# GpSimd computes the low half of 100 of the 504 weight pieces, where VectorE computed all of them

## The chip, the cores and the metric

The kernel runs on one core of one Trainium2 chip. The metric is the device time of one launch in microseconds (us). The names of the engines in the profile are PE (TensorE, matrix multiply) with PEld (its weight load), DVE (VectorE), ACT (ScalarE), POOL (GpSimd) and SP (SyncE, which here only starts DMAs).

## What is computed

Two transformer-like blocks run one after the other on 256 tokens of width 2048, all in float32. Of the reference only the products with large weights matter here:

```
# first block, twice (l = 0, 1)
mod = c_act @ w_mod[l] + b_mod[l]            # one row times 2048 x 6144
h = rmsnorm(x, norm_gain[l]) * (1.0 + scale) + shift
proj = h @ w_in[l]                           # 256 x 2048 times 2048 x 7504
...                                          # sparse attention, retention, gates
x = x + gate * (y @ w_out[l])                # 256 x 2048 times 2048 x 2048
# second block, once
h = concat([meta_tokens (16), x, pad])
proj = rms_norm(h, norm_mix) @ w_in_2        # 2048 x 7176
...                                          # stick-breaking and forgetting attention
h = h + merged @ w_out_2
q = rms_norm(h, norm_ffn) @ peer_w_query     # 2048 x 2048
...                                          # top-k, gather of 16384-row tables peer_u, peer_v
```

## The kernel before, in words

A float32 product is made from rounded halves. A weight piece `raw` is split into a high half `hi`, rounded to the engine's fp32r type, and a low half `lo = raw - hi`. The activations are split the same way (`hH`, `hL`). TensorE then makes three products for each pair: wH with hH, wL with hH, wH with hL (all at L1818, a helper that records every matmul; L1821 records the transposes).

**Seven passes.** `PIECES` lists the weight pieces: pass 0 (`w_in[0]`, 128 pieces), 1 (`w_out[0]`, 32), 2 (`w_in[1]`, 128), 3 (`w_out[1]`, 32), 4 (`w_in_2`, 120), 5 (`w_out_2`, 32) and 6 (`peer_w_query_2`, 32), together 504. A piece is 256 rows of the weight by a group of columns, mostly 512 wide, and lies in SBUF as 128 x 1024. Eight pieces (`pc` 0 to 7) make one column group.

**The road of a piece k.** SP loads it into `ring` (`NS` = 4 slots). ACT copies it, rounded, into `wH[k % 3]` (L626); for that it waits until TensorE has finished piece k - 3 (`"cut used"`, `NB` = 3 buffers). DVE subtracts into `wL[k % 3]` (L1130), which gives `"lo"` to TensorE and `"ring used"` to SP. In pass 4 the 16 meta tokens read some groups (keys and values of both attentions, and the last 344 columns) straight from the raw piece, so there `"ring used"` comes from TensorE.

**The order.** `order()` is one list of steps that every engine walks, each picking what concerns it. After TensorE's piece q comes the split of piece q + 3 (`splits`), then one or more steps of three lanes (`pump`): X (sparse attention, gates), Y (retention) and M (`mods`, the modulation rows). DVE carries most of the lane work between its splits. An engine's queue is strictly in order, so a lane step behind a split waits for it. The mods step on DVE (L1286) multiplies a 128 x 1024 piece of `w_mod` by a column of c and adds it to an accumulator in `UHM`. TensorE does so for pieces 0 to 63 of the 192, DVE for pieces 64 to 191; the latter are loaded by POOL (L2371, into `P` or `SY`, three slots), where the load of piece m + 3 stands at the same step as the use of piece m and waits for that use (`"mod used"`).

**POOL before the change** only starts DMAs: inputs, `w_mod`, the decay tables of the retention (L2347), and in the last part, from about 1800 us on, the indirect gathers of expert rows (L2361). In that last part DVE takes a dot product of each gathered 128 x 2048 tile of `peer_u` (L1777), and TensorE mixes the rows of `peer_v`.

Of the kernel before, what the change touches and what calls it, by code (L numbers as in the profile page):

```python
# [9 lines left out]
ALU = mybir.AluOpType  # L10
ACT = mybir.ActivationFunctionType
F32 = mybir.dt.float32
# [56 lines left out]
class Marks:  # L69
# [9 lines left out]
    def tick(self, sem, *names):  # L79
        self.n[sem] += 1  # L80
        return self._named(sem, 1, names)
# [13 lines left out]
    def at(self, *name):  # L95
        if self.counting:
            return None, 0
        sem, n = self.names[name]
        return self.handles[sem], n
# [60 lines left out]
PIECES = [[(n, c0, w, pc) for n, (c0, w) in enumerate(g) for pc in range(8)] for g in GROUPS]  # L160
NB, NS, NG = 3, 4, 11
# [3 lines left out]
def meta_part(c0, w):  # L165

    for a, b in ((SK, MSK), (SV, MSV), (FK, MFK), (FV, MFV)):
        if a <= c0 < a + 1024:
            return 0, b + c0 - a
    if c0 + w > FL:  # L170
        return FL - c0, MFL
    return None


def order():
# [198 lines left out]
def mixer_peer_program(nc, I, out):  # L374
    with ExitStack() as ctx:
# [8 lines left out]
        ring = sb("ring", [128, NS, 1024])  # L384
# [34 lines left out]
        handles = {}  # L419
        for name in ("pe_piece", "pe_turned", "pe_bias", "pe_side",  # L420
                     "act_hi", "act_stored", "act_x", "act_y", "act_h", "act_side",
                     "dve_lo", "dve_stored", "dve_x", "dve_y", "dve_h", "dve_side",
                     *[f"mod_in{i}" for i in range(11)], "const_in", "pos_in", "x_in", "meta_in", "forget_in", "ffn_in", "decay_in", "turned_in", "out_done", "out_act_done",
                     *[f"ring_in{i}" for i in range(NS)], *[f"expert_in{i}" for i in range(NG)]):
            handles[name] = sem(name)
# [66 lines left out]
        def heads(v, n):  # L492
            return v.rearrange("p (h n) -> p h n", h=n)
# [606 lines left out]
        def vector(e, w):  # L1100
# [20 lines left out]
            def split(p, q):  # L1121
                n, c0, wd, pc = PIECES[p][q]
                r, k = next(loads), next(cut)
                raw = heads(ring[:, r % NS, 0:2 * wd], 2)
                hi, lo = (heads(b[k % NB][:, 0:2 * wd], 2) for b in (wH, wL))
                w.wait_ge(*at("hi", k))
                names = [("lo", k)]
                if not (p == 4 and meta_part(c0, wd)):
                    names.append(("ring used", r))
                tt(lo, raw, hi.bitcast(F32), ALU.subtract).then_inc(*tick("dve_lo", *names))  # L1130
# [581 lines left out]
            for what, *a in order():  # L1712
# [41 lines left out]
                elif what == "meta":  # L1754
                    p, q = a
# [585 lines left out]


        def gpsimd(e, w):
            gathers = itertools.count()

            def load(sem, to, src, *names):
                e.dma_start(to, src).then_inc(*landed(sem, *names))  # L2347

            def gather(tab, picks):
                n = next(gathers)  # L2350
                slot, before = SLOTS[n]
                if before is not None:
                    w.wait_ge(*at("expert used", before))
                elif slot in (3, 4):
                    w.wait_ge(*at("turned x"))
                    w.wait_ge(*at("hidden", slot - 3))
                elif slot == 5:
                    w.wait_ge(*at("lo", LAST_CUT))
                elif slot == 7:
                    w.wait_ge(*at("grouped", 6, 3))  # L2360
                e.indirect_dma_start(gs[slot], None, tab[0], bass.IndirectOffsetOnAxis(ap=picks, axis=0)).then_inc(  # L2361
                    *landed(f"expert_in{slot}", ("gathered", n)))

            def mod_load(m):
                l, c0, k = m // 96, m // 16 % 6 * 1024, m % 16
                b, before = mod_slot(m)
                if before is not None:
                    w.wait_ge(*at("mod used", before))
                if m in (64, 160):
                    w.wait_ge(*at("chunk", 2 * l if m == 160 else 0, 3))  # L2370
                e.dma_start(mod_in[b], I["w_mod"][l, k * 128:(k + 1) * 128, c0:c0 + 1024]).then_inc(  # L2371
                    *landed(f"mod_in{b}", ("mod", m)))

            def mods(b0, b1):
                first, last = 16 * b0, 16 * b1
                if b0:
                    mod_load(first)
                    mod_load(first + 1)
                    mod_load(first + 2)
                for m in range(first, last):  # L2380
                    if b0 and m + 3 < last:
                        mod_load(m + 3)
                    yield
                    if b0 and m % 16 == 15:
                        yield
                        yield

            def meta_sum(p, n):
                yield

            def retention(l, half):
                for g in (2 * half, 2 * half + 1):
                    if (l, g) != (0, 0):
                        w.wait_ge(*at("decayed", *((l, g - 1) if g else (l - 1, 3))))
                    load("decay_in", dmt, I["dm"][:, 2 * g:2 * g + 2, :].rearrange("p h n -> p (h n)"), ("decay", l, g))
                    for _ in range(7):
                        yield

            lanes = Lanes({"mods": mods, "meta_sum": meta_sum, "retention": retention})
            for what, *a in order():  # L2400
                if what == "setup":
                    load("pos_in", posr, I["positions"][0, :].partition_broadcast(128))
                    for t in range(2):
                        load("pos_in", posc[:, t:t + 1], I["positions"][0, t * 128:(t + 1) * 128].rearrange("(p a) -> p a", a=1))
                    w.wait_ge(*at("bias cleared"))
                    for q in range(4):
                        load("pos_in", poss[32 * q:32 * q + 32, :], I["positions"][0, 64 * q:64 * q + 64].partition_broadcast(32))
                        load("pos_in", rb[32 * q:32 * q + 32, 8 * q:8 * q + 8], I["rel_bias"])
                        load("pos_in", rb0[32 * q + 1:32 * q + 32, 8 * q:8 * q + 8], I["rel_bias"][0:31, :],
                             *([("positions",)] if q == 3 else []))  # L2410
                    load("x_in", x[:, :, :], x_d, ("x",))
                elif what == "open":
                    lanes.open(*a)
                elif what == "step":
                    lanes.step(*a)
                elif what == "drain":
                    lanes.drain(*a)
                elif what == "meta":
                    p, q = a
                    if PIECES[p][q][3] == 7:  # L2420
                        lanes.open("M", "meta_sum", p, PIECES[p][q][0])
                elif what == "meta_in":
                    w.wait_ge(*at("chunk", 3, 3))
                    load("meta_in", P[0:16, 0, D:2 * D], I["meta_tokens_2"], ("meta tokens",))
                    load("forget_in", bf, I["b_forget_2"].rearrange("a h -> (a h)").partition_broadcast(128), ("forget bias",))
                elif what == "late_loads":
                    w.wait_ge(*at("grouped", 5, 0, 0))
                    load("ffn_in", nf, I["norm_ffn_2"][0, :].partition_broadcast(128), ("ffn gain",))
                    load("turned_in", MI[:, 912:1168], I["cw"][:, NCW:NCW + 256], ("places",))
                    w.wait_ge(*at("x added", 5, 3, 1))  # L2430
                    for t in range(2):
                        for q in range(4):
                            load("turned_in", P[q:128:4, 0, t * D:(t + 1) * D], x[32 * q:32 * q + 32, t, :],
                                 *([("turned x",)] if (t, q) == (1, 3) else []))
                elif what == "dot":
                    i, j = a
                    if (i, j) == (0, 0):
                        w.wait_ge(*at("chunk", 6, 3))
                    w.wait_ge(*at("experts", i, j // 16))
                    gather(I["peer_u_2"], ix[i % 4][:, j:j + 1])  # L2440
                elif what == "vmix":
                    i, b = a
                    w.wait_ge(*at("experts turned", i))
                    for m in range(b, 32, 8):
                        gather(I["peer_v_2"], ixT[i % 4][:, m:m + 1])
# [35 lines left out]
```

## Time and profile before

| what | us |
|---|---|
| median of 3 runs (3127.49 to 3130.35) | 3127.76 |
| span of the profiled execution, first to last instruction | 3121.8 |
| PE busy | 2089.0 |
| DVE busy | 1836.5 |
| ACT busy | 853.8 |
| POOL busy | 800.9 |

The profiled execution has no time of its own beside its span; the median of the runs is 5.96 us above the span, which is taken for what lies around it. "Busy" is the time in which an engine executes at least one instruction. The page's strip of 40 slices shows two parts: up to about 1800 us PE is nearly full and the DMA engines are not, and after that the DMA engines are full (9 or 8 in every slice) and PE has 2 or 3 tenths.

### The profile page before, as it was taken

To read this page: it belongs to the slowest core of one execution; us is meant where nothing else is said; L and a number is where in the kernel's file an instruction comes from. 1 tells how busy PE (TensorE), PEld (TensorE's weight loads), DVE (VectorE), ACT (ScalarE), POOL (GpSimd) and SP (SyncE) were. 2 spreads that over 40 slices of the span, in tenths; PEclk is the share of its full clock that TensorE was granted. 3 is DMA by queue.
4 is the path that set the end of the run, shared out by engine and by line. 5 is a ranking of instruction groups with operands and counts; after the bars stand their busy time and mean duration, and the time that the engine had idled before them with its cause. 6 is when DMAs were issued, how large, how long until landed. Compare 5 with 4: busy or idle time off the path is not lost.

```text
span 3121.8 us, 29077 instructions
## 1 busy us (share of the span) xinstructions
PE 2089.0 (67%) x11378; PEld 1478.6 (47%) x11378; DVE 1836.5 (59%) x2711; ACT 853.8 (27%) x1267; POOL 800.9 (26%) x680
## 2 busy tenths in 40 slices
PE   5888989989999999999999983223232322322235
PEld 2676777888787787666668871000000000000001
DVE  3679886566776664343336697766565555564430
ACT  1334544444454454544545420000000000000000
POOL 1111110000000000000000036665555555555552
PEclk8999999999999999999999996566656566666667
DMA  9887875557665545334226699999999999999998
GB/s 385 289 293 263 296 259 150 184 182 248 210 189 153 164 158 172 111 122 132 85 82 201 194 377 403 422 422 421 421 422 421 422 421 419 421 421 421 421 421 346
DMA packets 244741, 900.90 MB, mean 289 GB/s; under 512 B 20759, under 2 KB 45613, under 8 KB 178413
## 3 DMA queue, kind: packets, MB, share of 16 engines
q0 software_dynamic: 94208, 612.85, 48.9%
q1 hardware_dynamic: 149152, 284.53, 27.8%
q8 instruction: 90, 1.47, 0.2%
q10 hardware_dynamic: 1244, 1.67, 0.2%
q14 instruction: 47, 0.38, 0.0%
HBM read 894.78 MB, written 2.10 MB: 287 GB/s over the span
## 4 chain that ended last, share of the span: by engine, by line
PE 45%; DMA 29%; DVE 10%; ACT 3%; issue 3%; POOL 2%; ACTq 0%; POOLq 0%; DVEq 0%
PE pp L1818 38%; DMA late<-in_peer_v,MI 9%; DMA P<-in_peer_v,MI 5%; PE tp L1818 5%; DMA x<-in_peer_v,MI 5%; DMA ring<-in_peer_v,MI 4%; DVE wL L1130 3%; DMA SY<-in_peer_v,MI 2%; PE tp L1821 2%; ACT wH L626 1%; DMA ring<-in_peer_w_query 1%; DVE UHM L1286 1%; DMA ring<-in_w_in 1%; POOL late L2361 1%; DVE P L1777 0%
## 5 line engine op out<-in xcount | busy, mean ns | idle before, releaser
L1130 DVE TENSOR_TENSOR wL<-ring,wH 128x1024 fp32r<-128x1024 f32 (+3 forms) x504 | 583.2, 1161 | 573.7 <-ACT wH L626 572.4
L1818 PE MATMUL pp<-wH,hH 128*128 128x512 f32 (+3 forms) x1888 | 745.7, 395 | 35.5 <-DVE wL L1130 19.4
L1818 PE MATMUL pp<-wL,hH 128*128 128x512 f32 (+3 forms) x1888 | 721.4, 382 | 0.0
L1818 PE MATMUL pp<-wH,hL 128*128 128x512 f32 (+3 forms) x1888 | 720.5, 382 | 0.0
L626 ACT ACTIVATE wH<-ring 128x1024 fp32r<-128x1024 f32 (+3 forms) x504 | 508.3, 1011 | 729.7 <-PE pp L1818 548.0
L1818 PE MATMUL pp<-late,S 128*32 128x512 f32 x768 | 232.6, 879 | 335.7 <-DMA x<-in_peer_v,MI 156.3
L1818 PEld LDWEIGHTS pp<-wH,hH 128*128 128x128 f32 x1888 | 362.3, 192 | 141.2 <-issue 46.3
L1818 PEld LDWEIGHTS pp<-wH,hL 128*128 128x128 f32 x1888 | 361.6, 192 | 64.1
L1818 PEld LDWEIGHTS pp<-wL,hH 128*128 128x128 f32 x1888 | 362.8, 192 | 57.3 <-issue 1.0
L1777 DVE CUSTOM_DVE_ANT_0 late<-late,P 128x2048 f32<-128x2048 f32 x84 | 191.2, 2288 | 155.2 <-DMA late<-in_peer_u,MI 155.2
L1818 PE MATMUL pp<-P,S 128*32 128x512 f32 x360 | 162.7, 898 | 166.9 <-DMA late<-in_peer_v,MI 93.2
L1818 PEld LDWEIGHTS pp<-late,S 128*32 128x32 f32 x768 | 52.1, 154 | 441.3 <-issue 441.3
L1818 PE MATMUL pp<-ring,S 128*32 128x512 f32 x344 | 156.7, 890 | 142.3 <-DMA late<-in_peer_v,MI 142.3
L1818 PE MATMUL pp<-x,S 128*32 128x512 f32 x376 | 165.1, 880 | 126.2 <-DMA P<-in_peer_v,MI 65.8
L2371 POOL DMA_DIRECT2D P<-in_w_mod x85 | 44.9, 529 | 634.2 <-DVE hL L1173 314.3
L1818 PE MATMUL pp<-SY,S 128*32 128x512 f32 x200 | 140.3, 867 | 89.8 <-DMA P<-in_peer_v,MI 89.8
L1029 ACT ACTIVATE MI<-MI 128x32 f32<-128x32 f32 x8 | 1.8, 229 | 640.3 <-DVE MI L1697 640.3
L1777 DVE CUSTOM_DVE_ANT_0 P<-P 128x2048 f32<-128x2048 f32 x53 | 121.0, 2288 | 93.4 <-DMA P<-in_peer_u,MI 93.2
L2361 POOL DMA_INDIRECT late<-in_peer_v,MI x96 | 117.6, 1225 | 173.5 <-PE pp L1818 149.4
L1777 DVE CUSTOM_DVE_ANT_0 x<-x,P 128x2048 f32<-128x2048 f32 x49 | 111.9, 2289 | 78.9 <-DMA x<-in_peer_u,MI 78.9
L2347 POOL DMA_DIRECT2D UHM<-in_norm_ffn x1 | 0.5, 533 | 605.6 <-PE pp L1818 605.6
L1777 DVE CUSTOM_DVE_ANT_0 ring<-ring,P 128x2048 f32<-128x2048 f32 x47 | 107.2, 2288 | 75.7 <-DMA ring<-in_peer_u,MI 75.7
(305 smaller groups left out, 2985.2 us busy)
## 6 DMA issues: line engine op xcount, KB each, us to landing
ring<-in_w_in SPq DMA_DIRECT2D x288, 512.0 KB, 4.4
ring<-in_w_out SPq DMA_DIRECT2D x96, 512.0 KB, 4.2
P<-in_w_mod POOLq DMA_DIRECT2D x85, 512.0 KB, 5.1
late<-in_w_mod SPq DMA_DIRECT2D x64, 512.0 KB, 9.4
SY<-in_w_mod POOLq DMA_DIRECT2D x43, 512.0 KB, 5.5
ring<-in_w_in SPq DMA_DIRECT2D x48, 368.0 KB, 4.8
ring<-in_peer_w_query SPq DMA_DIRECT2D x32, 512.0 KB, 7.9
ring<-in_w_in SPq DMA_DIRECT2D x24, 344.0 KB, 3.2
```

What stands on the lines that cost most here:

```text
L626: act(heads(wH[k % NB][:, 0:2 * wd], 2), raw, ACT.Copy).then_inc(*tick("act_hi", ("hi", k)))
L1029: act(c3, c3, ACT.Exp).then_inc(*tick("act_x", ("gap exp", i)))
L1130: tt(lo, raw, hi.bitcast(F32), ALU.subtract).then_inc(*tick("dve_lo", *names))
L1286: stt(mod_acc, wv, c, mod_acc, ALU.mult, ALU.add).then_inc(*tick("dve_side", *names))
L1777: e.tensor_tensor_reduce(out=gs[slot], in0=gs[slot], in1=hn[i // 4], scale=1.0, scalar=0.0, op0=ALU.mult, op1=ALU.add, accum_out=aa[i % 2] ...
L1818: return e.matmul(o, l, r, start=start, stop=stop, skip_group_check=skip)
L1821: return e.transpose(o, i, ident[0:k, 0:k])
L2347: e.dma_start(to, src).then_inc(*landed(sem, *names))
L2361: e.indirect_dma_start(gs[slot], None, tab[0], bass.IndirectOffsetOnAxis(ap=picks, axis=0)).then_inc(*landed(f"expert_in{slot}", ("gathere ...
L2371: e.dma_start(mod_in[b], I["w_mod"][l, k * 128:(k + 1) * 128, c0:c0 + 1024]).then_inc(*landed(f"mod_in{b}", ("mod", m)))
```

## The change

A function `by_pool(p, q)` picks pieces: passes 0 to 5, every fourth piece of a pass (`q % 4 == 3`, thus `pc` 3 and 7 of each column group), and in pass 4 only where the group isn't one that the meta tokens read. These are 32 + 8 + 32 + 8 + 12 + 8 = 100 pieces: 80 of 512 columns, 12 of 368, 4 of 344 and 4 of 256. For these DVE skips its subtraction and POOL issues the same one, with the same operands and after the same wait for `hi`. It ticks a semaphore of its own, `pool_lo`, on which TensorE (`"lo"`) and SP (`"ring used"`) then wait.

```diff
+def by_pool(p, q):
+
+    return p < 6 and q % 4 == 3 and not (p == 4 and meta_part(*PIECES[p][q][1:3]))
...
                 hi, lo = (heads(b[k % NB][:, 0:2 * wd], 2) for b in (wH, wL))
+                if by_pool(p, q):
+                    return
                 w.wait_ge(*at("hi", k))
...
         def gpsimd(e, w):
+            loads, cut = itertools.count(), itertools.count()
+
+            def split(p, q):
+                wd = PIECES[p][q][2]
+                r, k = next(loads), next(cut)
+                if by_pool(p, q):
+                    raw, hi, lo = ring[:, r % NS, 0:2 * wd], wH[k % NB][:, 0:2 * wd], wL[k % NB][:, 0:2 * wd]
+                    w.wait_ge(*at("hi", k))
+                    e.tensor_tensor(lo, raw, hi.bitcast(F32), ALU.subtract).then_inc(
+                        *tick("pool_lo", ("lo", k), ("ring used", r)))
...
             for what, *a in order():
-                if what == "setup":
+                if what == "split":
+                    split(*a)
+                elif what == "sub_keys":
+                    next(loads), next(loads)
+                elif what == "setup":
```

In the rows of the instruction order, lines after the new function are 5 to 18 higher: L1130 is L1137, L1286 is L1293, L2371 is L2389, and L2359 is the new subtraction.

DVE's queue in pass 0 at pieces 59 to 61, before. `wL2<-ring,wH2` with its wait on `act_hi` is the subtraction of piece 59; `UHM<-...` is a mods step:

```order
L1296 TENSOR_TENSOR mcol<-tp0,bcol 128x2x4 [waits pe_turned]
L1105 TENSOR_SCALAR UHM<-P,cact 128x1024 [waits pe_side,dve_side,mod_in9]
L1130 TENSOR_TENSOR wL2<-ring,wH2 128x1024 [waits act_hi]
L1286 SCALAR_TENSOR_TENSOR UHM<-SY,cact,UHM 128x1024 [waits dve_side,mod_in10]
L1130 TENSOR_TENSOR wL0<-ring,wH0 128x1024 [waits act_hi]
L1286 SCALAR_TENSOR_TENSOR UHM<-P,cact,UHM 128x1024 [waits dve_side,mod_in8]
L1130 TENSOR_TENSOR wL1<-ring,wH1 128x1024 [waits act_hi]
```

The same place after:

```order
L1303 TENSOR_TENSOR mcol<-tp0,bcol 128x2x4 [waits pe_turned]
L1110 TENSOR_SCALAR UHM<-P,cact 128x1024 [waits pe_side,dve_side,mod_in9]
L1293 SCALAR_TENSOR_TENSOR UHM<-SY,cact,UHM 128x1024 [waits dve_side,mod_in10]
L1137 TENSOR_TENSOR wL0<-ring,wH0 128x1024 [waits act_hi]
L1293 SCALAR_TENSOR_TENSOR UHM<-P,cact,UHM 128x1024 [waits dve_side,mod_in8]
L1137 TENSOR_TENSOR wL1<-ring,wH1 128x1024 [waits act_hi]
```

The subtraction of piece 59 is gone from DVE, and the two mods steps around it now follow each other directly.

POOL's queue at the same place (from piece 55 to piece 63), before:

```order
L2371 DMA SY<-in_w_mod 128x1024 [waits dve_side]
L2371 DMA P<-in_w_mod 128x1024 [waits dve_side] x2
L2371 DMA SY<-in_w_mod 128x1024 [waits dve_side]
L2371 DMA P<-in_w_mod 128x1024 [waits dve_side] x2
L2371 DMA SY<-in_w_mod 128x1024 [waits dve_side]
```

and after:

```order
L2389 DMA SY<-in_w_mod 128x1024 [waits dve_side]
L2359 TENSOR_TENSOR wL1<-ring,wH1 128x1024 [waits act_hi]
L2389 DMA P<-in_w_mod 128x1024 [waits dve_side] x2
L2359 TENSOR_TENSOR wL2<-ring,wH2 128x1024 [waits act_hi]
L2389 DMA SY<-in_w_mod 128x1024 [waits dve_side]
L2389 DMA P<-in_w_mod 128x1024 [waits dve_side] x2
L2389 DMA SY<-in_w_mod 128x1024 [waits dve_side]
L2389 DMA P<-in_w_mod 128x1024 [waits dve_side]
L2359 TENSOR_TENSOR wL0<-ring,wH0 128x1024 [waits act_hi]
```

The subtractions of pieces 55, 59 and 63 now stand between the loads of `w_mod`, behind a load that waits for DVE's last mods step.

## Rows read from the trace of the kernel before

**Rows 1.** The page: span, and the strips of PE and of the DMA engines.

```profile
span 3121.8 us, 29077 instructions
...
PE   5888989989999999999999983223232322322235
...
DMA  9887875557665545334226699999999999999998
```

**Rows 2.** Busy time by stretch: pass 0, pass 2, the part after pass 6.

```profile
core 0: us, PE busy (x) PEld busy (x) DVE busy (x) ACT busy (x) POOL busy (x), PEclk, DMA share, GB/s
98.00:552.00 454.00, 397.59 (x1967) 333.84 (x1965) 360.93 (x510) 193.82 (x283) 52.89 (x100) 0.95 0.75 251
...
642.00:1060.00 418.00, 388.79 (x1943) 331.26 (x1942) 292.76 (x458) 195.87 (x288) 19.06 (x36) 0.97 0.63 193
...
1876.00:3121.00 1245.00, 379.70 (x2128) 104.44 (x2128) 683.26 (x1001) 25.73 (x36) 684.90 (x490) 0.64 1.00 416
```

**Rows 3.** Waits of PE from 98 to 1750 us: total, times, longest.

```profile
PE pp L1818 <- DVE wL L1130: 19.4, 17, 3.4
PE tp L1821 <- DVE S L1347: 12.8, 2, 8.9
PE tp L1821 <- DVE P L1324: 10.7, 2, 8.0
```

**Rows 4.** The chain of work that ended last, from 291 us: start, us, what.

```profile
291.54 0.06 DVE wL L1130
...
292.59 1.28 DVE UHM L1286
...
367.20 1.13 DVE wL L1130
368.34 0.33 DVE SY L1462
...
958.02 1.14 DVE wL L1130
...
1709.63 27.23 PE pp L1818 x120
```

**Rows 5.** The same chain at a piece of pass 2 whose split follows ACT.

```profile
928.80 1.07 ACT wH L626
...
929.89 1.22 DVE wL L1130
```

**Rows 6.** The line L1130: ns min/median/max, first and last start, forms.

```profile
L1130 DVE TENSOR_TENSOR wL<-ring,wH x504: 683/1225/1228, 98.3 to 1875.5; 128x1024 fp32r<-128x1024 f32 x139, 128x736 fp32r<-128x736 f32 x16, 128x688 fp32r<-128x688 f32 x8, 128x512 fp32r<-128x512 f32 x5
```

**Rows 7.** Timeline from 2199 us, POOL's gathers, then DVE's dot products: start, us, instruction, [idle].

```profile
2200.28 2.18 POOL L2361 DMA_INDIRECT P<-in_peer_u,MI  x1 [0.30 <-issue]
2202.77 0.93 POOL L2361 DMA_INDIRECT ring<-in_peer_u,MI  x1 [0.30 <-issue]
...
2214.67 2.70 POOL L2361 DMA_INDIRECT late<-in_peer_v,MI  x1 [6.00 <-PE pp L1818]
...
2199.36 2.29 DVE L1777 CUSTOM_DVE_ANT_0 late<-late,P 128x2048 f32<-128x2048 f32 x1 [0.19 <-DMA late<-in_peer_u,MI]
...
2214.27 2.29 DVE L1777 CUSTOM_DVE_ANT_0 P<-P 128x2048 f32<-128x2048 f32 x1 [0.18 <-DMA P<-in_peer_u,MI]
```

**Rows 8.** POOL's loads of `w_mod`: one line's ns, then the median us to landing.

```profile
L2371 POOL DMA_DIRECT2D P<-in_w_mod x85: 528/528/542, 121.4 to 873.5; - x85
...
SY<-in_w_mod POOLq DMA_DIRECT2D x43, 512.0 KB, 5.5
```

**Rows 9.** DVE's waits for those loads: total, times, longest.

```profile
DVE UHM L1286 <- DMA SY<-in_w_mod: 7.6, 6, 1.6
DVE UHM L1286 <- DMA P<-in_w_mod: 6.1, 6, 1.3
```

**Rows 10.** Timeline of POOL at the loads of `w_mod` near 291 us.

```profile
291.83 0.53 POOL L2371 DMA_DIRECT2D P<-in_w_mod  x1 [11.01 <-DVE UHM L1105]
294.16 0.53 POOL L2371 DMA_DIRECT2D SY<-in_w_mod  x1 [1.80 <-DVE UHM L1286]
```

More of the change, by code:

```diff
@@ L421, in mixer_peer_program @@
                      "act_hi", "act_stored", "act_x", "act_y", "act_h", "act_side",
-                     "dve_lo", "dve_stored", "dve_x", "dve_y", "dve_h", "dve_side",
+                     "pool_lo", "dve_lo", "dve_stored", "dve_x", "dve_y", "dve_h", "dve_side",
                      *[f"mod_in{i}" for i in range(11)], "const_in", "pos_in", "x_in", "meta_in", "forget_in", "ffn_in", "decay_in", "turned_in", "out_done", "out_act_done",
```

## Prediction, made before the changed kernel was timed

> **What bounds the kernel now.** I began with the page. Its strips [rows 1] show two kernels in one: up to about 1800 us PE is nearly full, after that the DMA engines are. In the second part, from 1876 us, the DMA share is 1.00 [rows 2]; no moved subtraction lies there (they end with pass 5), so that part only starts earlier or later as a whole. The question is the time at which pass 5 ends.
>
> Next the table of stretches [rows 2]. A piece of 512 columns costs PE 27.23 / 10 = 2.72 us where PE runs unhindered (the last row of the group, ten pieces of 12 matmuls [rows 4]). Pass 0 has 128 pieces, 24 of them only 368 wide, and takes 454 us, with DVE busy for 361 and PE idle for 454 - 397.6 = 56.4. Pass 2 has the same pieces and takes 418 us, DVE 293, PE idle 29.2. So pass 0 is where DVE presses on PE: its lane work and mods steps share one queue with the splits. The table of PE's waits [rows 3] gives the form of it: 19.4 us in 17 waits for a low half, and larger ones for lane results that DVE delivers late.
>
> Last the chain of work that ended last, from 291 us, where its record begins. In passes 0 to 5 it goes through 76 of the 504 splits. 18 of those are among the 100 moved ones: 14 follow a DVE instruction with no idle time (pieces 59, 63, 67, 71, 79, 95, 99, 115 of pass 0 and 35, 59, 63, 79, 95, 99 of pass 2; first, one between and last in [rows 4]), and 4 follow ACT's high half (91 of pass 0; 71, 91 and 115 of pass 2; one of them in [rows 5]). Before 291 us the chain shows nothing; in the timeline of DVE 11 moved splits of that stretch (7 to 31, 39, 47, 51, 55) stand without idle time too. 25 moved splits on a saturated DVE, then, and 4 behind ACT. The other 71 lie where DVE has time, and their removal alone gives nothing.
>
> **The change part by part.**
>
> *DVE loses 100 subtractions.* On the chain one takes 1.14 us [rows 4], 1.22 by itself [rows 6]. If nothing else happened: 14 x 1.14 = 16.0 us for the chain, 11 x 1.14 = 12.5 us before 291 us, together 28.5 at most.
>
> *The four behind ACT.* There DVE stood idle until the high half was ready, 1.07 us, and then subtracted, 1.22 us [rows 5]. Without its split DVE runs its lane steps in that time: up to 4 x 2.3 = 9.2 us.
>
> *POOL's subtraction.* No row shows one. It can't be quicker than DVE's 1.22 us [rows 6]. For the other end I take the two inputs one after the other, 2 x 1.22 = 2.45 us; it is also near the 2.29 us that DVE takes for two inputs of twice the length [rows 7]. I take 2.45. The Trainium skill (page GPSIMD Engine Reference, section Performance versus the Vector engine) gives 4497 ns against 2293 for a float32 tensor_tensor of 2048 elements; an estimate from that page is 1.22 x 1.96 = 2.4 us, and the sum would be the same.
>
> *Do the two engines hold each other up?* POOL's gather takes 0.93 us alone and 2.18 or 2.70 us where DVE's two-input dot product is running: the first, begun at 2200.28, ends 0.8 us after DVE's at 2201.65; the second, begun at 2214.67, ends 0.8 us after DVE's at 2216.56 [rows 7]. So POOL, which reads its indices from SBUF, stands until DVE's two-input instruction is over, and then needs its own time. No row shows the other direction, since POOL's reads there are tiny. The price for DVE of a moved split thus lies between -1.14 us (DVE never waits) and -1.14 + 2.45 = +1.31 us (DVE waits for all of it). The instructions behind a moved split are mostly mods steps, rotations and splits with two SBUF inputs [rows 4], which speaks for the upper end; some (the top-k steps, reads of PSUM) have one such input and run beside. I take 1.8 us of waiting, the 2.45 less half of a 1.2 us instruction that is already under way, thus +0.66 us a piece. The Trainium skill (page SBUF — State Buffer, section SBUF: two separate sides) says that the pair of ports is locked for a whole instruction, against VectorE instructions with two SBUF inputs too; the trace agrees for POOL with its 2.18 and 2.70 us. By that rule DVE would wait for all of the 2.45.
>
> For the 14 on the chain that is 14 x 0.66 = 9.2 us. Of the 11 before 291 us I count half, as no chain shows that the end hangs on them: 5.5 x 0.66 = 3.6. The four behind ACT: DVE gains up to 2.3 and then waits 1.8, so 4 x -0.5 = -2.
>
> *PE gets those low halves later.* In a clean stretch the high half of piece k starts when PE ends piece k - 3, and PE wants the low half two pieces later, 2 x 2.72 = 5.44 us. Then 1.07 + 2.45 = 3.5 us is in time and costs nothing; the cover is 1.9 us. It is gone where DVE is late, which are PE's 17 waits [rows 3]. A quarter of them, 4, would be on moved pieces, each later by 2.45 - 1.22 = 1.2 us: +5 us. (Ends: 0, and with a DVE instruction held before each, 4 x 2.5 = 10.)
>
> *POOL's queue.* A moved subtraction stands behind a load of `w_mod` that waits for the last mods step, and in front of the next load. Near 291 us POOL is released by that step, spends 0.53 us on the load and only then comes to piece 59 [rows 10], at 292.36, when DVE before was near the end of it (it began right after 291.54 [rows 4]). The load behind it waits for the subtraction. Loads are issued three steps ahead and land 5.5 us later [rows 8]; at 2.33 us a step [rows 10] that is 7.0 us, so 1.0 us of cover after 0.53 + 5.5. DVE waits for such loads 12 times already, 13.7 us in all [rows 9]. A load late by up to 2.45 us runs over by up to 1.5; but the mods step that it waits for mostly comes later than POOL's subtraction. Ends 0 and 24 x 1.5 = 36 (the moved pieces that stand between mods steps of pass 0); near the lower one, since most loads have POOL idle for 1.8 us or more [rows 10]: I take +2. SP's reloads of `ring` are asked for four pieces ahead, some 11 us, and stay covered. The decay tables and the one wait for the meta tokens lie behind subtractions too, 9 issues, each with long idle time before: nothing.
>
> **Sum:** 9.2 + 3.6 - 2 + 5 + 2 = +17.8 us by full count. Some of what DVE loses early is made up by PE's next wait being shorter, as several of these pieces follow each other (59 to 71, 95 to 99) and end in one and the same wait; I leave off a quarter for that: +13 us. Span 3121.8 + 13 = 3134.8; with 5.96 us around the span: 3140.8.
>
> **The rivals.**
>
> *A. No contest for DVE: faster.* POOL waits for DVE but DVE not for POOL. For it: DVE's dot products keep 2.29 us whatever POOL does. Against: POOL's reads there are short. Then -28.5 - 9.2 = -37.7 at most; behind a shortened chain other chains come up (PE alone needs most of pass 0: its idle time is 56.4 us, and waits for lane results bound by ACT and PE stay), and late low halves cost +5 to +10. About -22 us: 3106.
>
> *B. It cancels.* DVE waits for about 1.1 us a piece, because it is often in an instruction with one SBUF input, or the four behind ACT and others like them give back what the rest costs: within 6 us, 3128.
>
> *C. Slower by a stall of PE at each moved piece.* This is the end on the far side of no change too, but steeper than my forecast. If POOL's subtraction, with its holds behind DVE, takes over 5.44 - 1.07 = 4.37 us, the cover above is gone everywhere and PE stands at each of the 100. At 5 us that is 100 x 0.6 = 63 us: 3190. Against: it needs over three times DVE's 1.22.
>
> *D. The change doesn't do what it says.* POOL passes a mods step only when DVE has, so it is never ahead of DVE in pass 0; DVE's queue gets shorter but the low half isn't there sooner. That is part of the forecast, and with a POOL starved by an unbroken DVE it goes to 3150.
>
> **How the numbers follow.** Forecast with D: 0.52 (3132 to 3152). A: 0.27. B: 0.16. C: 0.05. Predicted time 3141. Range: from the middle of A to the upper end of the forecast and a little beyond, 3105 to 3158, which leaves out a third of A's spread and C. A measurement of this kernel can tell about 0.2%, 6.3 us, from no change. Slower by more: 0.48 of the forecast's 0.52, plus C: 0.53. Faster by more: A and a little of B: 0.28. Within: 0.19.
>
> **What would show it.** POOL's TENSOR_TENSOR rows: about 2.4 us, longer where DVE is in a two-input instruction. DVE's L1293 (mods) and L1137 (splits), 1.28 and 1.22 us before, should be longer beside POOL's subtraction, or idle in front of it; if both keep their times and no gaps appear, A holds. Pass 0 should grow from 454 us by about 9, pass 2 by about 5, passes 1, 3, 4 and 5 by nothing. PE's waits for a low half should be on POOL. The prediction is wrong if pass 0 gets shorter, or if PE waits on POOL in the clean passes.

## The result, and the profile after

The changed kernel is slower: 3161.37 us (median of 4 runs, 3152.56 to 3168.87) against 3127.62 us (4 runs, 3125.19 to 3130.35). The ratio is 1.0112, with a 95% interval of 1.0088 to 1.0137: +33.7 us as the difference of the medians (+35.0 by the ratio). The forecast had the sign and the kind of loss, but said +13, and the measured time lies above its range. The profiled run took 3158.96 us with a span of 3157.3; so 1.7 us lie around the span, not the 5.96 that the prediction took. In every later run of the kernel before it is 1.9 to 2.1 us; the profiled execution of before was thus a quick one, of some 3124 us, and the two profiles differ by 35.5 us.

The page after, the lines that answer to [rows 1] and the busy line:

```profile
span 3157.3 us, 29079 instructions
...
PE 2102.5 (67%) x11378; PEld 1488.1 (47%) x11378; DVE 1798.5 (57%) x2611; ACT 853.9 (27%) x1267; POOL 1031.3 (33%) x780
```

DVE has 100 instructions less, but only 38.0 us less of busy time (1836.5 before), where 100 subtractions at their sizes are some 115 us. The table of stretches, cut at the same pieces as [rows 2] (pass 0, pass 2, the part after pass 6), with pass 4 between:

```profile
core 0: us, PE busy (x) PEld busy (x) DVE busy (x) ACT busy (x) POOL busy (x), PEclk, DMA share, GB/s
98.00:573.00 475.00, 409.05 (x1967) 341.61 (x1966) 368.36 (x478) 194.23 (x283) 127.05 (x132) 0.93 0.73 240
...
663.00:1094.00 431.00, 393.52 (x1943) 335.22 (x1942) 279.53 (x426) 195.42 (x288) 92.39 (x69) 0.96 0.60 187
...
1186.00:1691.00 505.00, 481.07 (x2389) 352.54 (x2388) 188.66 (x304) 247.18 (x394) 26.07 (x13) 0.97 0.38 117
...
1912.00:3157.00 1245.00, 378.53 (x2128) 103.65 (x2128) 683.49 (x1001) 25.73 (x36) 683.65 (x490) 0.64 1.00 415
```

Pass 0 grew from 454 to 475 us and pass 2 from 418 to 431, together 34 of the 35.5 us between the two spans. The last part kept its 1245 us. DVE's busy time in pass 0 went up, from 360.9 to 368.4, although 32 subtractions left it. PE's time splits in two: in the two passes its idle time grew by 9.5 and 8.3 us and its busy time by 11.5 and 4.7 us, for the same matmuls, at a granted clock of 0.93 and 0.96 instead of 0.95 and 0.97.

GpSimd's subtraction, the line L2359 of the changed kernel (ns min/median/max, first and last start):

```profile
L2359 POOL TENSOR_TENSOR wL<-ring,wH x100: 1264/2399/3445, 109.3 to 1780.8; 128x1024 fp32r<-128x1024 f32 x80, 128x736 fp32r<-128x736 f32 x12, 128x512 fp32r<-128x512 f32 x4, 128x688 fp32r<-128x688 f32 x4
```

The median is 2.40 us, as forecast (2.45). The timeline of the changed kernel at pieces 59 and 60, POOL's rows and then DVE's (start, us, instruction):

```profile
301.67 0.53 POOL L2389 DMA_DIRECT2D P<-in_w_mod  x1 [11.79 <-DVE UHM L1110]
302.21 2.78 POOL L2359 TENSOR_TENSOR wL<-ring,wH 128x1024 fp32r<-128x1024 f32 x1
304.94 0.57 POOL L2389 DMA_DIRECT2D SY<-in_w_mod  x1
...
301.47 1.29 DVE L1293 SCALAR_TENSOR_TENSOR UHM<-SY,cact,UHM 128x1024 f32<-128x1024 f32 x1
302.67 3.41 DVE L1137 TENSOR_TENSOR wL<-ring,wH 128x1024 fp32r<-128x1024 f32 x1
306.00 1.27 DVE L1293 SCALAR_TENSOR_TENSOR UHM<-P,cact,UHM 128x1024 f32<-128x1024 f32 x1
```

This is the direction that no row of before showed. GpSimd's instruction begins beside a mods step of DVE and takes 0.38 us longer than its 2.40. DVE's next split, of piece 60, is then held: GpSimd is done at 304.99, and the split ends 1.09 us after that, having taken 3.41 us instead of 1.22. The hold doesn't appear as a wait: it is inside the duration of the row, and counts as busy time. Over pass 0 the groups of DVE's instructions in the changed kernel (busy us, mean ns of one, idle before):

```profile
L1137 DVE TENSOR_TENSOR wL<-ring,wH 128x1024 fp32r<-128x1024 f32 x72 | 93.9, 1307 | 57.0 <-ACT wH L631 56.7
L1293 DVE SCALAR_TENSOR_TENSOR UHM<-P,cact,UHM 128x1024 f32<-128x1024 f32 x60 | 90.9, 1515 | 9.7 <-DMA P<-in_w_mod 8.5
L1293 DVE SCALAR_TENSOR_TENSOR UHM<-SY,cact,UHM 128x1024 f32<-128x1024 f32 x30 | 42.2, 1408 | 8.9 <-DMA SY<-in_w_mod 8.1
...
L1384 DVE MAX8 sm<-MI 128x8 f32<-128x256 f32 x8 | 3.4, 426 | 0.2
```

and the same four in the kernel before:

```profile
L1130 DVE TENSOR_TENSOR wL<-ring,wH 128x1024 fp32r<-128x1024 f32 x96 | 117.1, 1221 | 56.5 <-ACT wH L626 56.2
L1286 DVE SCALAR_TENSOR_TENSOR UHM<-P,cact,UHM 128x1024 f32<-128x1024 f32 x60 | 76.8, 1280 | 7.1 <-DMA P<-in_w_mod 6.1
L1286 DVE SCALAR_TENSOR_TENSOR UHM<-SY,cact,UHM 128x1024 f32<-128x1024 f32 x30 | 38.4, 1281 | 8.1 <-DMA SY<-in_w_mod 7.6
...
L1377 DVE MAX8 sm<-MI 128x8 f32<-128x256 f32 x8 | 3.4, 426 | 0.2
```

Splits and mods steps, with two inputs in SBUF, are stretched; the top-k step, with one, keeps its 426 ns, and all seven of these steps that begin inside a subtraction of GpSimd keep their length. One input is no safeguard by itself, though: seven `TENSOR_SCALAR` and one `COPY` that read and write SBUF were held as well, 11.1 us in all, of which this is one (0.17 us in the kernel before; GpSimd's subtraction runs from 909.78 to 912.17):

```profile
910.08 2.13 DVE L1110 TENSOR_SCALAR sm<-sm 128x4 f32<-128x4 f32 x1
```

Two rows of PE's waits after, from 98 to 1783 us, beside [rows 3]:

```profile
PE pp L1825 <- POOL wL L2359: 15.3, 11, 4.0
PE pp L1825 <- DVE wL L1137: 14.2, 11, 3.5
```

The 11 waits for GpSimd lie in pass 0 (13.7 us) and pass 2 (1.5 us), none in the other passes.

### The profile page after: what moved, and what is told of

It reads as the page before. It is cut to its first block, busy times and chain, and to the rows that moved or that the text cites. A ratio compares the mean times of both kernels' runs of the same rounds, so it can differ in the third digit from the quotient of the medians.

```text
span 3157.3 us, 29079 instructions
## 1 busy us (share of the span) xinstructions
PE 2102.5 (67%) x11378; PEld 1488.1 (47%) x11378; DVE 1798.5 (57%) x2611; ACT 853.9 (27%) x1267; POOL 1031.3 (33%) x780
## 4 chain that ended last, share of the span: by engine, by line
PE 44%; DMA 29%; DVE 8%; issue 3%; ACT 2%; POOL 2%; ACTq 0%; POOLq 0%; DVEq 0%
PE pp L1825 38%; DMA late<-in_peer_v,MI 9%; DMA P<-in_peer_v,MI 5%; PE tp L1825 5%; DMA x<-in_peer_v,MI 5%; DMA ring<-in_peer_v,MI 4%; DMA SY<-in_peer_v,MI 2%; DVE wL L1137 2%; DMA ring<-in_peer_w_query 2%; PE tp L1828 2%; ACT wH L631 1%; DMA ring<-in_w_in 1%; DVE UHM L1293 1%; POOL late L2379 1%; POOL x L2379 0%
## 5 line engine op out<-in xcount | busy, mean ns | idle before, releaser
L1137 DVE TENSOR_TENSOR wL<-ring,wH 128x1024 fp32r<-128x1024 f32 (+3 forms) x404 | 483.8, 1201 | 614.7 <-ACT wH L631 614.1
L1825 PE MATMUL pp<-wH,hH 128*128 128x512 f32 (+3 forms) x1888 | 750.7, 398 | 49.0 <-POOL wL L2359 15.3
L2359 POOL TENSOR_TENSOR wL<-ring,wH 128x1024 fp32r<-128x1024 f32 (+3 forms) x100 | 231.3, 2313 | 1075.6 <-ACT wH L631 1075.0
L2379 POOL DMA_INDIRECT late<-in_peer_u,MI x84 | 129.9, 1547 | 25.6 <-issue 25.3
```

What stands on the lines that cost most here:

```text
L1825: return e.matmul(o, l, r, start=start, stop=stop, skip_group_check=skip)
L2359: e.tensor_tensor(lo, raw, hi.bitcast(F32), ALU.subtract).then_inc(*tick("pool_lo", ("lo", k), ("ring used", r)))
```

## The experiments

Times are against the kernel before, run on the same chip; a difference in us is that of the ratio, and the brackets hold its 95% interval. Theory 1 says that the loss is GpSimd's instruction itself (the holds at SBUF, late low halves, TensorE's clock in the added waits), theory 2 that it is GpSimd's in-order queue (late `w_mod` loads, slow hand-over).

### Relief alone, and the queue alone

The first kernel lets nobody compute the 100 low halves:

```diff
                 if by_pool(p, q):
...
-                    e.tensor_tensor(lo, raw, hi.bitcast(F32), ALU.subtract).then_inc(
-                        *tick("pool_lo", ("lo", k), ("ring used", r)))
...
-                act(heads(wH[k % NB][:, 0:2 * wd], 2), raw, ACT.Copy).then_inc(*tick("act_hi", ("hi", k)))
+                more = [("lo", k), ("ring used", r)] if by_pool(p, q) else []
+                act(heads(wH[k % NB][:, 0:2 * wd], 2), raw, ACT.Copy).then_inc(*tick("act_hi", ("hi", k), *more))
```

> Left out: the 100 moved low halves are computed by nobody (wL keeps that of an older piece); TensorE and SyncE take ACT's high half as the sign. It is the most that relieving DVE can give. Theory 1 (the loss of 33.7 us comes from GpSimd's instruction itself: DVE and GpSimd hold each other up at SBUF, low halves come late, and TensorE's clock falls in the added waits): faster than before by 10 to 30 us, pass 0 shorter by 8 to 20. Theory 2 (the loss comes from the queue: GpSimd's in-order waits delay the w_mod loads and the hand-over): the same for this run. If it is within 4 us of before, DVE's relief is worth nothing and rival A of the prediction could never have come.

Measured: 3106.16 us against 3126.26, ratio 0.9943 (0.9922 to 0.9965), -17.8 us (-24.4 to -10.9). The second keeps every wait, signal and queue position of the changed kernel, but shrinks the instruction:

```diff
-                    e.tensor_tensor(lo, raw, hi.bitcast(F32), ALU.subtract).then_inc(
+                    e.tensor_tensor(lo[:, 0:2], raw[:, 0:2], hi[:, 0:2].bitcast(F32), ALU.subtract).then_inc(
```

> Left out: GpSimd subtracts only the first 2 of the columns of each moved piece; every wait, signal and queue position is that of the changed kernel. Theory 1: as fast as the run in which nobody computes them, within 6 us, since an instruction of about 0.1 us neither holds DVE nor comes late. Theory 2: still slow, at least half of the 33.7 us.

Measured: 3110.07 us, 0.9954 (0.9935 to 0.9973), -14.4 us. The two intervals overlap for most of their length, so a cost of the waits in the queue can't be told from nothing, and theory 2, which wanted at least half of the loss here, falls. GpSimd's instruction takes only 0.20 us in this kernel; the queue with its time taken up as well is tested further down, by the fills. Relieving DVE is worth 14 to 18 us. The table of stretches for pass 0 and pass 2 in the first of them (columns as above):

```profile
98.00:542.00 444.00, 394.97 (x1966) 332.77 (x1965) 327.93 (x479) 193.40 (x283) 52.87 (x100) 0.96 0.77 257
632.00:1039.00 407.00, 383.56 (x1938) 327.26 (x1937) 258.47 (x425) 195.00 (x286) 19.06 (x36) 0.98 0.63 198
```

DVE is busy for 327.9 and 258.5 us there, with the same instructions that take 368.4 and 279.5 us in the changed kernel. The differences, 40.4 and 21.1 us, are the holds: 1.26 us for each of the 32 moved pieces of pass 0, 0.66 us in pass 2. DVE's waits for `w_mod` loads in this kernel, up to the end of pass 5, beside [rows 9]:

```profile
DVE UHM L1294 <- DMA P<-in_w_mod: 14.5, 13, 2.0
DVE UHM L1294 <- DMA SY<-in_w_mod: 10.4, 7, 2.4
```

They are 24.9 us here and 13.7 before: of what DVE is relieved, 11 us turn into waiting for loads.

### Contention without relief

DVE computes all 504 low halves, TensorE waits for DVE alone, and GpSimd subtracts the (dead) raw piece from itself:

```diff
-                    w.wait_ge(*at("hi", k))
-                    e.tensor_tensor(lo, raw, hi.bitcast(F32), ALU.subtract).then_inc(
-                        *tick("pool_lo", ("lo", k), ("ring used", r)))
+                    w.wait_ge(*at("lo", k))
+                    e.tensor_tensor(raw, raw, raw, ALU.subtract).then_inc(*tick("pool_lo", ("ring used", r)))
```

> DVE computes all 504 low halves as before and TensorE waits for it alone; GpSimd in addition runs a two-input subtraction of the same size on the same 100 pieces, in place on the raw piece (which is dead then), right after DVE's. Extra work that nobody needs, but which uses SBUF. Theory 1: the contention without any relief: slower than before by more than the changed kernel, 35 to 60 us, with DVE's rows stretched as in the changed kernel (mods steps up to 3.8 us). Theory 2: TensorE never waits for GpSimd here, so at most +8 us.

Measured: 3172.43 us, 1.0143 (1.011 to 1.0175), +44.7 us. Nobody waits for GpSimd's results except the ring's next load (ACT's waits for the loads of `w_in` are 126.6 us in this kernel and 121.8 before), and still this is the slowest kernel of all, though its interval overlaps that of the changed one. Its GpSimd instruction takes 1.90 us, and DVE's mods steps are held in it too, though up to 2.9 us and not to the 3.8 expected (per source line: ns min/median/max, first and last start, forms):

```profile
L2357 POOL TENSOR_TENSOR ring<-ring x100: 1054/1895/3207, 110.5 to 1797.3; 128x1024 f32<-128x1024 f32 x80, 128x736 f32<-128x736 f32 x12, 128x512 f32<-128x512 f32 x4, 128x688 f32<-128x688 f32 x4
...
L1291 DVE SCALAR_TENSOR_TENSOR UHM<-P,cact,UHM x80: 1254/1279/2912, 133.5 to 934.6; 128x1024 f32<-128x1024 f32 x80
```

The median step is untouched and the longest takes 2.9 us: a few are held for long, most not at all.

### Lateness without reads, and one input

GpSimd only writes, twice:

```diff
-                    e.tensor_tensor(lo, raw, hi.bitcast(F32), ALU.subtract).then_inc(
-                        *tick("pool_lo", ("lo", k), ("ring used", r)))
+                    e.memset(lo.bitcast(F32), 0.0).then_inc(*tick("pool_lo"))
+                    w.wait_ge(*now("pool_lo"))
+                    e.memset(lo.bitcast(F32), 0.0).then_inc(*tick("pool_lo", ("lo", k), ("ring used", r)))
```

> Changes the computation: instead of subtracting, GpSimd fills the low half of the 100 moved pieces with zeros, twice (it writes SBUF and reads nothing), at the same place and with the same waits. It is there for lateness without reads: about 2 us from high half to signal. If the loss of 55 us between the run in which nobody computes and the changed kernel is mostly DVE being held by GpSimd's reads, this run is near before: -15 to -2 us, with DVE's mods steps at their 1.28 us. If late low halves make most of it, +15 to +35 us. If GpSimd's writes hold DVE as much as its reads, the mods steps are stretched here too.

Measured: 0.9947 (0.9929 to 0.9966), -16.6 us, the gain of pure relief within its interval, and a little more than the -15 to -2 expected. The source line of the first of the two fills in its trace (the second, L2361, has the same median), then that of DVE's mods step (ns min/median/max, first and last start):

```profile
L2359 POOL MEMSET wL<- x100: 524/953/977, 109.1 to 1734.5; 128x1024 f32 x80, 128x736 f32 x12, 128x512 f32 x4, 128x688 f32 x4
...
L1293 DVE SCALAR_TENSOR_TENSOR UHM<-P,cact,UHM x80: 1251/1280/1287, 130.9 to 881.1; 128x1024 f32<-128x1024 f32 x80
```

No mods step is longer than 1.290 us (1.287 in this row), no split longer than 1.229, and 42 of them ran beside a fill for over 0.3 us: GpSimd's writes hold nobody. GpSimd's queue is taken up for about 1.9 us a piece here, so this run answers theory 2 too. And low halves that come some 1.9 us after the high half cost almost nothing, though PE's table shows 12.1 us of waits for them here (11 waits, against 15.3 us in the changed kernel). Those waits replace others: in pass 0 PE is idle for 47.4 us here and for 49.0 where nobody computes the pieces.

One input instead of two:

```diff
-                    e.tensor_tensor(lo, raw, hi.bitcast(F32), ALU.subtract).then_inc(
+                    e.tensor_copy(lo, raw).then_inc(
```

> Changes the computation: GpSimd copies the raw piece into wL (one SBUF input) instead of subtracting, at the same place with the same waits. Theory 1: its instruction takes half the time (1.1 to 1.4 us instead of 2.40), DVE is held for half as long and no low half is late by much: between the run in which nobody computes and the changed kernel, -10 to +10 us against before. Theory 2: as slow as the changed kernel.

Measured: 0.9999 (0.9985 to 1.0014). The copy takes 1.05 us, and it eats the whole gain of the relief: one input in SBUF is enough for GpSimd to hold DVE, for a shorter time. The copy's source line in that kernel's trace, and the group of DVE's mods steps (busy us, mean ns of one):

```profile
L2359 POOL CAST wL<-ring x100: 615/1046/2099, 109.4 to 1746.5; 128x1024 fp32r<-128x1024 f32 x80, 128x736 fp32r<-128x736 f32 x12, 128x512 fp32r<-128x512 f32 x4, 128x688 fp32r<-128x688 f32 x4
...
L1293 DVE SCALAR_TENSOR_TENSOR UHM<-P,cact,UHM 128x1024 f32<-128x1024 f32 x60 | 83.7, 1395 | 10.4 <-DMA P<-in_w_mod 9.6
```

### Where it costs

Six kernels differ from the changed one only in the line that picks the pieces. The first three:

```diff
-    return p < 6 and q % 4 == 3 and not (p == 4 and meta_part(*PIECES[p][q][1:3]))
+    return p == 0 and q % 4 == 3
```

> Only the 32 pieces of pass 0 are moved. If the loss belongs to the places where DVE is saturated, pass 0 alone carries 21 us of the 33 (its growth in the profile of the changed kernel), and passes 1 to 6 keep their lengths. If the loss is a price per moved piece, a third of it: 11 us.

```diff
+    return p == 2 and q % 4 == 3
```

> Only the 32 pieces of pass 2 are moved. By place: 13 us (7 to 16). By a price per piece: 11 us. With the run of pass 0 it tells whether the two add up to the whole.

```diff
+    return p in (1, 3, 4, 5) and q % 4 == 3 and not (p == 4 and meta_part(*PIECES[p][q][1:3]))
```

> Only the 36 pieces of passes 1, 3, 4 and 5 are moved, where TensorE waits little. By place: within 4 us of before; TensorE is never later for a low half that takes 2.4 us after 1.07 us of ACT, against 5.4 us of cover. By a price per piece: 12 us.

Measured: pass 0 alone 1.0049 (1.0031 to 1.0067), +15.3 us; pass 2 alone 1.0040 (1.0023 to 1.0056), +12.5 us; the four others 0.9999 (0.9984 to 1.0015), nothing. It is a matter of place, not a price per piece: 36 pieces in clean passes cost nothing and gain nothing, where a price per piece asked for +12 us. The runs of pass 0 and of pass 2 alone don't tell the two apart, since the 11 us of such a price lie within both intervals. The two add up to 28 of 33.7 us, within their intervals. In its profile the run of pass 0 needs 471 us for it, close to the 475 of the changed kernel, but with PE busy for 401 at a clock of 0.95 and not 409 at 0.93:

```profile
98.00:569.00 471.00, 401.02 (x1965) 334.60 (x1965) 366.98 (x479) 193.77 (x283) 125.98 (x132) 0.95 0.74 242
```

The other three look into pass 0 and at the kind of lane work:

```diff
+    return p == 0 and q < 56 and q % 4 == 3
```

> Only the 14 moved pieces of pass 0 before piece 56 (piece 3 to 55), the stretch for which the record of the chain is missing. The prediction counted half of 11 of them, +3.6 us. If they are all priced by DVE's holds, +8 to +10 us, which is what that stretch grew by in the changed kernel (193 to 203 us).

```diff
+    return p == 0 and q >= 56 and q % 4 == 3
```

> Only the 18 moved pieces of pass 0 from piece 56 on (59 to 127), 9 of which the chain of before names. If only pieces on the chain cost, 8 x 0.66 = +5 us; if a hold costs wherever DVE has little slack, +8 to +11 us, the growth of that stretch in the changed kernel (261 to 272 us). Together with the first stretch they should give the +13.6 us of the run with the 32 pieces of pass 0.

```diff
+    return (p == 0 and 40 <= q < 60 or p == 2 and 48 <= q < 68) and q % 4 == 3
```

> Only 10 pieces: those of the stretches of passes 0 and 2 in which DVE's lane work is the top-k selection (pieces 43 to 59 of pass 0, 51 to 67 of pass 2), whose instructions read one tensor and needn't wait for GpSimd. If single-input work makes the move worthwhile there, -3 to -8 us; if the splits and mods steps between them are held all the same, -2 to +5 us.

Measured: before piece 56 1.0019 (1.0003 to 1.0035), +5.9 us; from piece 56 on 1.0031 (1.0015 to 1.0047), +9.7 us, together 15.6, as the run of all 32. For the stretch without a record of the chain 3.6 us were counted; the +5.9 us can't tell that from the +8 to +10 of the other reading, as its interval runs from +0.9 to +10.9. The top-k pieces 1.0027 (1.001 to 1.0045), +8.4 us for only 10 pieces. Its profile has only some 3 us of this in passes 0 and 2, so the size is unsure, and it lies above both expectations; that nothing is gained there is clear. One row shows an instance, four instructions of the lane X just outside the top-k itself (start, us for all four):

```profile
259.10 4.66 DVE L1377 SCALAR_TENSOR_TENSOR MI<-S,P,MI 128x256 f32<-128x256 f32 x4
```

The four take 2.04 us in the kernel before; here GpSimd's subtraction starts at 260.02 for 2.40 us, and one of them stands through it.

## Why the prediction was right in kind and short in size

**What bounds, and where.** Right: all of the growth is in passes 0 and 2, none in 1, 3, 4, 5 or in the last part (f3_clean: 0.9999). Their sizes were 9 and 5 us in the forecast and are 21 and 13 in the profile.

**GpSimd's instruction.** Right: 2.40 us measured, 2.45 taken.

**The relief: the step that failed.** The sum has 14 x 1.14, 5.5 x 1.14 and 4 x 2.3, together 31.4 us, for what DVE is rid of. With nobody computing the pieces the gain is 17.8 us, and its interval (10.9 to 24.4) doesn't reach 31.4; the tiny instruction and the fills, 14.4 and 16.6 us, say the same. These 13.6 us are the largest part of the 20.7 by which the forecast fell short. By pass the sum gives 17.7 us for pass 0 and 13.7 for pass 2, and the profile of that run shows 10 and 11. What a chain names is what is late now; once that is quicker, something else is late. Here DVE's waits for `w_mod` loads grew by 11 us. That they are what ate the relief is read from one profile, and no run shows it. The prediction reckoned in this way for rival A (-22 us, from which late low halves were already taken), and didn't in its own sum.

**The quarter left off** for holds that end in one wait, 4.8 us, had no row behind it, and nothing measured asks for it.

**The holds and the other costs.** Right that DVE is held in turn. By full count the sum has 42.3 us of holds (23.5 x 1.8), 5 for late low halves and 2 for the queue, 49.3 together. Measured, the change less the relief is 33.7 + 17.8 = 51.5 us. The agreement is in part luck, since terms that are too large and too small make up for each other. To see this, every DVE row of the changed kernel was set against the same row of the kernel before, and what it took longer given to the subtraction of GpSimd beside it. That makes 62.2 us for passes 0 and 2 (61.5 by the tables above):

| moved pieces of passes 0 and 2 | holds counted | holds in the profile |
|---|---|---|
| 14 on the chain, behind DVE | 25.2 | 25.0 |
| 4 on the chain, behind ACT | 7.2 | 1.5 |
| 11 before 291 us | 9.9 (half of them) | 13.7 |
| 35 others | 0 | 22.0 |

The price of 1.8 us a piece was right where DVE is saturated: 25.0 / 14 = 1.79. Wrong was to put the others at nothing, since "the other 71 lie where DVE has time": 35 of them lie in passes 0 and 2 and held DVE for 22 us. How much of these 22 us reaches the end no run tells; the 36 pieces in the clean passes held DVE for 9 us and cost nothing. So holds counted and holds that delay the end are two things, and only their sum with the rest, 51.5 us, is measured.

**Late low halves and the queue.** Sized at +5 and +2. Filling instead of subtracting leaves pure relief at 0.9947 against 0.9943, and the tiny instruction at 0.9954: about 1 and 3 us, neither clear of nothing.

**TensorE's clock** was not in the sum. In the changed kernel's profile 16.2 of the 34 us that passes 0 and 2 grew are PE busy longer for the same matmuls. Each added stall is a stretch in which TensorE does nothing, and the granted clock, an average over its levels of 1.2 and 2.4 GHz, is lower in the same stretches. The part of pass 0 up to piece 59, before and after:

```profile
98.00:291.00 193.00, 162.38 (x847) 141.66 (x845) 155.44 (x225) 76.29 (x102) 26.96 (x51) 0.93 0.81 274
```

```profile
98.00:301.00 203.00, 169.80 (x848) 146.94 (x847) 158.52 (x211) 76.65 (x102) 55.90 (x65) 0.91 0.78 261
```

Of the 10 us of growth 7.4 are PE's busy time, at 0.91 instead of 0.93. GpSimd's subtractions by themselves don't stretch the matmuls: in pass 1, with 8 of them and the clock at 1.00, PE is busy for 89.56 us before and after. That this share isn't fixed is seen in the run of pass 0 alone (471 us at 0.95: PE busy +3.4 and idle +13.6). Which part of the loss is clock and which is waiting thus differs from one execution to the next; no run here held the clock and kept the stalls, so the 16 us are read from one profile, not shown by an experiment.

**The rivals.** A (no contest for DVE) and B (it cancels) are refuted by the 3.41 us row and by contention without relief. C needed over 4.37 us for GpSimd's instruction; its longest is 3.45. D was right as a description: POOL comes to piece 59 at 302.21, only after the mods step of DVE that its load waits for (L1110).

## What to carry to other kernels

Before moving elementwise work from a saturated VectorE to GpSimd, count a hold of up to GpSimd's full duration for every VectorE instruction beside it that needs two inputs from SBUF (here some with one as well), in every stretch in which VectorE is short of time, and don't count the relief by the chain alone; here 2.4 us of GpSimd bought 1.2 us of VectorE and lost more. Where VectorE had time, 36 moved pieces changed nothing. Work in which GpSimd only writes held nobody here. And in a kernel that lives from TensorE, price a new stall above its length, since the granted clock was lower too where stalls were added (one profile's reading, not an experiment's).

## What the runs showed of the hardware

- GpSimd's two-input subtraction of 128x1024 float32 takes 2.40 us, a copy 1.05 us, a fill 0.95 us, a subtraction with both inputs the same tensor 1.90 us (medians).
- The hold goes both ways and hides in the duration: a VectorE split of 1.22 us took 3.41, a GpSimd gather of 0.93 us took 2.70 [rows 7]. The Trainium skill (page SBUF — State Buffer, section SBUF: two separate sides) says that the pair of ports is kept for a whole instruction; the 3.41 us agree, and by that rule DVE's wait would have been taken as 2.4 and not 1.8 us. The mean over the 14 pieces on the chain is 1.79 us, and single holds go up to 2.6 us.
- A fill on GpSimd held no mods step and no split (longest 1.290 and 1.229 us); the copy, with one input, did (mean of a mods step 1.395 us).
- On VectorE's side the top-k steps, with one input, were not held (426 ns), while `TENSOR_SCALAR` and `COPY` from SBUF to SBUF were (0.17 us became 2.13).
- A pass that an edit doesn't touch varies between profiles: pass 4 took 507, 512, 506 and 509 us (before, i1_early, i2_rest, i3_topk), with the granted clock at 0.96, 0.95, 0.96 and 0.96. Differences of 5 us can't be read from one profile of this kernel.
